# Down projection of a decoder block as seven block products with a three-slot ring

## The chip, the cores and the metric

The kernel runs on one core of one Trainium2 chip. The metric is the time of one execution in microseconds (us) on the device. The engines are TensorE (PE, with its weight loads PEld), VectorE (DVE), ScalarE (ACT), GpSimd (POOL) and SyncE (SP), whose queue issues nearly all DMAs here.

## What is computed

A decoder block on 2048 tokens of width 1024: two mixers side by side, one output projection, then a SwiGLU feed-forward with 2816 hidden columns and a last norm. The part at hand, all in float32:

```python
h = h + jnp.concatenate([y_a, y_b], axis=-1) @ w_out[l]
u = rmsnorm(h, ln2_g[l])
h = h + (jax.nn.silu(u @ w_gate[l]) * (u @ w_up[l])) @ w_down[l]
return rmsnorm(h, final_g)
```

## The kernel before

Tokens go in four blocks (it) of 512 through the mixers. The feed-forward works on pairs (p) of such blocks, so on 1024 tokens; the program order is `ffn(0), down, down, ffn(1), down, down`.

**Precision.** Every float32 product is three matmuls: each operand is split into a rounded part (hi, written by ScalarE) and the rest (lo, written by VectorE as raw minus hi), and hi x hi, lo x hi and hi x lo are added up in a PSUM bank.

**Gate and up (`ffn`).** For each of 22 iterations g of a pair (even g gate, odd g up, so 11 gate-and-up pairs j) the product of a 256-column block of the weights with the 1024 tokens is built from seven block products (A11, A12, S2, S1, S3, S4, A22) of 12 matmuls each. GpSimd forms the sums of weight blocks. ScalarE and VectorE split the weights of a product three products ahead (LEAD): after product o of g they handle the weights of product o + 3. VectorE and ScalarE read the banks into four quarters, gq0 to gq3 for gate, au0 to au3 for up; ScalarE applies silu to gq, VectorE multiplies au by gq, and SP stores au into the DRAM scratch a_scr.

**Down (`down(it)`).** For each of the four 512-token blocks, 22 rows k are taken in order. A row has 128 rows of w_down (1024 columns, 512 KB, dw_raw) and the activations that go with them (512 tokens, 256 KB, da_raw), and gives 24 matmuls: four groups of 128 tokens by two halves of columns, so all eight PSUM banks. Three buffers of each kind form a ring (CRING = 3). SP loads row rr into its slot when TensorE has finished row rr - 3 (`load_row`, the wait on s_row); ScalarE writes the hi parts (`row_hi`), VectorE the lo parts (`row_lo`), both two rows ahead in their programs; TensorE waits for lo. Between rows SP loads the operands of the next pair's gate and up from u_scr, 1 MB each, and in the next rows VectorE combines and splits them. After the 22 rows eight additions bring the banks into the residual (`residual`), and squares, their sum, a root and a scaling give the output.

**Order.** Nothing is scheduled by a planner: each engine's program is written out by these functions, engines run in order, and semaphores join them. A waiting instruction holds up all behind it on its engine.

## Time and profile before

| | us |
|---|---|
| median of 3 runs | 2338.1 |
| lowest, highest | 2337.46, 2338.29 |
| the profiled execution | 2335.22 |
| its span, first to last instruction | 2333.5 |
| mixers, up to about | 1000 |
| gate and up, first pair, up to | 1411.76 |
| down, first pair, up to | 1657.59 |
| gate and up, second pair, up to | 2078.87 |
| down, second pair, last matmul | 2321.81 |

The profile is one execution, taken by the hardware profiler. Matmuls overlap one another, so the time of a stretch is read from starts, not from durations. Idle time of an engine that nobody waits for costs nothing. In the rows below SPq is SP's DMA queue, and a bracket at the end of a row says how long the engine sat idle before it and what ended that.

### The profile page before, as it was taken

What the parts mean: (1) busy time and instruction counts of PE and PEld (TensorE: products, weight loads), DVE (VectorE), ACT (ScalarE), POOL (GpSimd) and SP (SyncE); (2) the same over time, 40 slices, a digit from 0 to 9 for tenths busy, and PEclk for the clock granted to TensorE, in tenths of its full rate; (3) what the DMA queues carried; (4) which work ended last, traced back from release to release, by engine and by line L of the source; (5) the groups of instructions that cost most, each with busy time, mean ns of one, the idle gap of its engine ahead of it and who ended that gap; (6) DMA issues with size and microseconds to landing.
All of it is one profiled execution on the core that took longest, in us unless ns stands there. A gap on an engine that the chain in (4) does not pass through costs nothing.

```text
span 2333.5 us, 29887 instructions
## 1 busy us (share of the span) xinstructions
PE 2272.5 (97%) x11336; PEld 1886.6 (81%) x11336; DVE 1355.0 (58%) x2047; ACT 981.0 (42%) x1727; POOL 478.4 (21%) x376
## 2 busy tenths in 40 slices
PE   6999999999999999899999999999999999999998
PEld 5888788878887888678888888778888888888786
DVE  5775588557865786656554544753555555543444
ACT  4554545444544554443333333532433333332422
POOL 1230223122222122332222320000222223200000
PEclk9999999999999999999999999999999999999999
DMA  4222332233323323523232216646232222235463
GB/s 118 83 81 81 109 110 92 94 104 118 96 86 106 103 89 117 183 73 113 86 127 73 91 55 245 229 136 235 90 105 82 93 84 84 81 109 192 138 212 126
DMA packets 217854, 269.87 MB, mean 116 GB/s; under 512 B 12784, under 2 KB 164336, under 8 KB 214896
## 3 DMA queue, kind: packets, MB, share of 16 engines
q1 hardware_dynamic: 215408, 259.58, 33.8%
q10 hardware_dynamic: 2304, 8.39, 0.9%
q8 instruction: 91, 1.49, 0.3%
q14 instruction: 51, 0.42, 0.1%
HBM read 219.69 MB, written 48.23 MB: 115 GB/s over the span
## 4 chain that ended last, share of the span: by engine, by line
PE 81%; DVE 7%; issue 3%; ACT 3%; DMA 3%; POOL 1%; SPq 1%; ACTq 0%; DVEq 0%; POOLq 0%
PE M L1050 9%; PE M L1052 9%; PE M L1051 9%; PE M L758 7%; PE M L760 6%; PE M L759 6%; PE M L1080 3%; PE M L1082 3%; PE M L1081 3%; PE X L1081 3%; PE X L1080 3%; PE X L1082 3%; PE X L1050 3%; PE X L1052 3%; PE X L1051 2%
## 5 line engine op out<-in xcount | busy, mean ns | idle before, releaser
L1536 DVE TENSOR_TENSOR wlo<-raw,whi 128x1024 fp32r<-128x1024 f32 x120 | 161.8, 1348 | 216.9 <-ACT whi L1110 216.9
L758 PE MATMUL M<-uhi,whi 128*128 128x512 f32 x704 | 283.9, 403 | 1.7 <-DVE ulo L1558 1.5
L760 PE MATMUL M<-uhi,wlo 128*128 128x512 f32 x704 | 275.4, 391 | 0.0
L759 PE MATMUL M<-ulo,whi 128*128 128x512 f32 x704 | 274.8, 390 | 0.0
L1950 DVE TENSOR_TENSOR dw_lo<-dw_raw,dw_hi 128x1024 fp32r<-128x1024 f32 x88 | 108.0, 1228 | 263.2 <-ACT dw_hi L1443 262.9
L1050 PE MATMUL M<-t_hi,wu_hi 128*128 128x512 f32 x616 | 240.1, 390 | 1.6 <-DVE wu_lo L1871 0.9
L1052 PE MATMUL M<-t_hi,wu_lo 128*128 128x512 f32 x616 | 240.0, 390 | 0.0
L1051 PE MATMUL M<-t_lo,wu_hi 128*128 128x512 f32 x616 | 239.7, 389 | 0.0
L1443 ACT ACTIVATE dw_hi<-dw_raw 128x1024 fp32r<-128x1024 f32 x88 | 93.3, 1061 | 313.0 <-DMA dw_raw<-in_w_down_dram 309.8
L1871 DVE TENSOR_TENSOR wu_lo<-fraw,wu_hi 128x512 fp32r<-128x512 f32 x132 | 133.1, 1018 | 111.6 <-ACT wu_hi L1386 111.2
L1110 ACT ACTIVATE whi<-raw 128x1024 fp32r<-128x1024 f32 x120 | 126.6, 1055 | 156.4 <-PE M L760 140.2
L2088 POOL TENSOR_TENSOR pr<-pr,rd 128x512 f32<-128x512 f32 x64 | 84.4, 1318 | 386.6 <-DVE rd L1569 386.6
L758 PEld LDWEIGHTS M<-uhi,whi 128*128 128x128 f32 x704 | 132.6, 188 | 32.5 <-issue 6.2
L760 PEld LDWEIGHTS M<-uhi,wlo 128*128 128x128 f32 x704 | 132.5, 188 | 28.7
L759 PEld LDWEIGHTS M<-ulo,whi 128*128 128x128 f32 x704 | 132.9, 189 | 25.7 <-issue 0.7
L1080 PE MATMUL M<-dw_hi,da_hi 128*128 128x512 f32 x352 | 137.5, 391 | 8.5 <-DVE da_lo L1950 4.5
L2154 POOL TENSOR_TENSOR fs<-fraw 128x512 f32<-128x512 f32 x44 | 58.4, 1328 | 411.7 <-DMA fraw<-in_w_gate_dram 207.3
L2160 POOL TENSOR_TENSOR fraw<-fraw,fs 128x512 f32<-128x512 f32 x44 | 57.4, 1304 | 409.9 <-DVE wl_lo L1871 409.8
L1871 DVE TENSOR_TENSOR wu_lo<-fs,wu_hi 128x512 fp32r<-128x512 f32 x88 | 61.2, 696 | 134.5 <-ACT wu_hi L1386 133.5
L1050 PEld LDWEIGHTS M<-t_hi,wu_hi 128*128 128x128 f32 x616 | 115.6, 188 | 26.9 <-DVE wu_lo L1871 2.1
L1082 PE MATMUL M<-dw_hi,da_lo 128*128 128x512 f32 x352 | 137.0, 389 | 0.0
L1081 PE MATMUL M<-dw_lo,da_hi 128*128 128x512 f32 x352 | 137.0, 389 | 0.0
(271 smaller groups left out, 5252.2 us busy)
## 6 DMA issues: line engine op xcount, KB each, us to landing
raw<-in_w_in_dram SPq DMA_DIRECT2D x88, 512.0 KB, 3.8
dw_raw<-in_w_down_dram SPq DMA_DIRECT2D x88, 512.0 KB, 3.7
fraw<-in_w_gate_dram SPq DMA_DIRECT2D x44, 512.0 KB, 4.6
fraw<-in_w_up_dram SPq DMA_DIRECT2D x44, 512.0 KB, 4.8
a_scr<-au SPq DMA_DIRECT2D x88, 256.0 KB, 2.0
da_raw<-a_scr SPq DMA_DIRECT2D x88, 256.0 KB, 3.9
raw<-in_w_out_dram SPq DMA_DIRECT2D x32, 512.0 KB, 3.8
xs<-in_x_dram SPq DMA_DIRECT2D x32, 256.0 KB, 4.1
```

Of the source, the lines that this page charges most:

```text
L758: mm(bank, whi[s][:, kb, :], hi, start=first, stop=False)
L759: mm(bank, whi[s][:, kb, :], lo, start=False, stop=False)
L760: return mm(bank, wlo[s][:, kb, :], hi, start=False, stop=last)
L1050: mm(bank[:, :], wh[:, k, :], hi[:, k, :], start=start and k == 0, stop=False, skip_group_check=True)
L1051: mm(bank[:, :], wh[:, k, :], lo[:, k, :], start=False, stop=False, skip_group_check=True)
L1052: last = mm(bank[:, :], wl[:, k, :], hi[:, k, :], start=False, stop=k == KH - 1, skip_group_check=True)
L1080: mm(DBANKS[n][:, :], ahi_k[:, tokens], whi_k[:, cols], start=k == 0, stop=False)
L1081: mm(DBANKS[n][:, :], ahi_k[:, tokens], wlo_k[:, cols], start=False, stop=False)
L1082: last = mm(DBANKS[n][:, :], alo_k[:, tokens], whi_k[:, cols], start=False, stop=k == KF - 1)
L1110: A(whi[s][:, :, :], raw[s][:, :, :], ACT.Copy).then_inc(s_hi[s], 1)
L1536: V.tensor_tensor(wlo[s][:, :, :], raw[s][:, :, :], whi[s][:, :, :].bitcast(F32), ALU.subtract).then_inc(s_lo[s], 1)
L1871: V.tensor_tensor(wl[:, :, :], ffn_part(g, o), wh[:, :, :].bitcast(F32), ALU.subtract).then_inc(s_flo, 1)
```

## The change

Down is computed for the 1024 tokens of a pair at once, with seven block products q in place of eight: two token halves by two column halves of the result, and w_down's 22 blocks of 128 rows taken as 11 pairs (j). Product q takes 11 rows, so a pair has 77 rows of 12 matmuls. A row is one 128x512 half block of weights (256 KB) and one 512-token block of activations (256 KB), side by side in one ring slot (ring0 to ring2), which ScalarE and VectorE each split with one instruction of 128x1024. There are still three slots.

- The activations' sums that the products need are formed in gate and up by VectorE: two after au2's product, two after au3's, written over gq1, gq2, au2 and gq3, and stored by SP. a_scr holds seven blocks for each j.
- The weights' combinations are formed once, in the first pair's `ffn`: from g = 10 on SP loads one 1 MB block of w_down (tw) after each g, VectorE makes four in-place sums in the next g (`t_step`, behind products A11, S2 and S1), and SP stores it into t_scr. From product 2 on, both pairs read weights from t_scr.
- TensorE writes a product into four banks, in two sets in turn. Banks are not cleared for every product (BEGINS); each product's banks are added into the residual during the next product (`residual`), four additions of 128x512 for each of seven products.
- The residual is loaded in 16 pieces of 256 KB, and the next pair's operands in 28 pieces of 256 KB in place of 7 loads of 1 MB, one at most behind a row. Squares, root, scaling and stores of the first 512 tokens of a pair are done before the last row.

```diff
+TARGET = ((0, 0), (0, 0), (0, 1), (1, 1), (1, 1), (0, 1), (1, 0))
+BEGINS = (0, 1, 3)
+WEIGHT_HALF = ((False, 0, 0), (False, 1, 0), (True, 0, 0), (True, 0, 1), (True, 1, 1), (False, 1, 1), (True, 1, 0))
+SQUARED = ((0, 0), (1, 1), (0, 1), (1, 0))
+SQUARED_WITH = (1, 4, 5, 6)
+PIECES = (("r", 0), "T3", "T1", ("r", 2), "T2", ("r", 1), "T4", "B11", "B21", ("r", 3), "B22")
+COMBINE_AT = {27: 0, 38: 1, 41: 2, 49: 3}
+SPLIT_AT = {51: "B11", 54: "B21", 59: "T2", 61: "T1", 63: "T3", 70: "B22", 75: "T4"}
...
+    a_scr = nc.dram_tensor("a_scr", [NPAIR, PRODUCTS, NJ, P, T], F32, kind="Internal").ap()
+    t_scr = nc.dram_tensor("t_scr", [KF, P, D], F32, kind="Internal").ap()
+    w_down_2 = w_down.rearrange("o (j k p) d -> (o j) p k d", k=2, p=P)
...
-        DW = [pair_at("dw0", stage_at, stage_at + 4 * K, (P, D)), pair_at("dw1", y_at + 4 * K, y_at + 8 * K, (P, D)),
-              pair_at("dw2", whi_at + 4 * K, wlo_at + 4 * K, (P, D))]
-        DA = [pair_at("da0", g1_at + 2 * K, spare_at, (P, T)), pair_at("da1", snap_at, snap_at + 2 * K, (P, T)),
-              pair_at("da2", gu_at, gu_at + 2 * K, (P, T))]
-        res = [at(f"res{b}", (P, D), kk_at + 4 * K * b) for b in range(TB)]
+        RING = [pair_at(f"ring{i}", o, o + 4 * K, (P, 2, T)) for i, o in enumerate((stage_at, y_at + 4 * K, snap_at))]
+        res = [[at(f"res0{b}", (P, D), o) for b, o in enumerate((dist_at, whi_at + 4 * K, wlo_at + 4 * K, gu_at))],
+               [at(f"res1{b}", (P, D), kk_at + 4 * K * b) for b in range(TB)]]
         gfrow = at("gfrow", (P, D), y_at + 28 * K)
-        dump = [snap[1], acc_last]
+        dump = acc_last
+        tw = [at(f"tw{i}", (P, 2, D), kk_at + 8 * K * i) for i in range(2)]
...
+        def banks_of(p, g):
+
+            return BANKS[(p + g) % 2]
+
+        def down_banks(p, q):
+
+            return BANKS[(p + q) % 2] + (X[2 + (p + q) % 2],)
...
-                sp.dma_start(OPERAND[o][2][:, :, :], u_scr[2 * p + n, :, k0:k0 + KH, :]).then_inc(s_opl[o], 16)
+                for k in range(KH) if part is None else (part,):
+                    sp.dma_start(OPERAND[o][2][:, k, :], u_scr[2 * p + n, :, k0 + k, :]).then_inc(s_opl[o], 16)
...
+                sp.dma_start(a_scr[p, (0, 6, 4, 1)[n], j, :, :], au[n][:, :]).then_inc(s_ast[n], 16)
+
+            def store_s(p, j, n):
+
+                sp.wait_ge(s_au, 7 * (p * NJ + j) + (4, 5, 7)[n])
+                sp.dma_start(a_scr[p, (3, 2, 5)[n], j, :, :], gq[1 + n][:, :]).then_inc(s_sst, 16)
+
+            def load_t(j):
+
+                if j < 2:
+                    sp.wait_ge(s_ust, 32 * NSB)
+                else:
+                    sp.wait_ge(s_ts, 16 * (j - 1))
+                sp.dma_start(tw[j % 2][:, :, :], w_down_2[j, :, :, :]).then_inc(s_tl, 16)
+
+            def store_t(j):
+
+                sp.wait_ge(s_tc, 4 * j + 4)
+                sp.dma_start(t_scr_2[j, :, :, :], tw[j % 2][:, :, :]).then_inc(s_ts, 16)
...
-                it, k = 2 * p + rr // KF, rr % KF
+                q, j = divmod(rr, NJ)
                 if rr >= CRING:
-                    sp.wait_ge(s_row, p * 2 * KF + rr - CRING + 1)
+                    sp.wait_ge(s_row, p * NR + rr - CRING + 1)
...
+                ring = RING[rr % CRING][2]
+                combined, k, half = WEIGHT_HALF[q]
+                if combined:
...
+                sp.dma_start(ring[:, 0, :], (t_scr if combined else w_down_k)[2 * j + k, :, half * T:(half + 1) * T]
+                             ).then_inc(s_ring[rr % CRING], 16)
...
+                sp.dma_start(ring[:, 1, :], a_scr[p, q, j, :, :]).then_inc(s_ring[rr % CRING], 16)
...
+                    if p == 0 and g >= T_LOAD + 2:
+                        store_t(g - T_LOAD - 2)
...
                         store_a(p, j, 1)
                         if last:
                             load_row(p, 1)
+                            load_row(p, 2)
+                        store_s(p, j, 0)
+                        store_s(p, j, 1)
                         store_a(p, j, 2)
                         store_a(p, j, 3)
+                        store_s(p, j, 2)
                     if p == 0 and g == 9:
                         store_u(NSB - 1, 0)
                         store_u(NSB - 1, 1)
-
...
+                    if p == 0 and 0 <= g - T_LOAD < NJ:
+                        load_t(g - T_LOAD)
+                if p == 0:
+                    store_t(NJ - 1)
...
+            def down(p):
+                pieces = {}
+                for i in range(TB * len(PIECES)):
+                    pieces[CRING + i * 29 // 20] = (PIECES[i // TB], i % TB)
+                for rr in range(CRING, NR):
+                    load_row(p, rr)
+                    if rr in pieces:
+                        what, part = pieces[rr]
+                        if what in OPERAND_NAMES:
+                            if p + 1 < NPAIR:
+                                load_operand(p + 1, OPERAND_NAMES[what], part)
+                        else:
+                            m, half = SQUARED[what[1]]
+                            load_res(p, m, part, half)
+                    if rr == 45:
                         for n in (2, 3):
                             sp.wait_ge(s_ast[n], 16 * NJ * (p + 1))
                         sp.dma_start(gfrow[:, :], final_g.partition_broadcast(P)).then_inc(s_gf, 16)
-                    if it % 2 and k == 9:
-                        store_out(it - 1)
-                    if k == 10:
-                        load_res(it)
-                    if it % 2 and k == 12 and p + 1 < NPAIR:
-                        load_ffn(p + 1, 0)
+                    if p + 1 < NPAIR and rr in (67, 70):
+                        load_ffn(p + 1, 0, (int(rr == 70),))
+                    if rr >= NR - 2:
+                        store_out(p, 0, rr - NR + 2)
+                for b in range(2, TB):
+                    store_out(p, 0, b)
...
+            def down(p):
+                for rr in range(NR):
+                    q, j = divmod(rr, NJ)
+                    banks = down_banks(p, q)
+                    pe.wait_ge(s_rowlo, NR * p + rr + 1)
+                    hi, lo, _ = RING[rr % CRING]
+                    for b in range(TB):
+                        if j == 0:
+                            wait_bank_read(pe, p, q, b)
+                        tokens = slice(b * P, (b + 1) * P)
+                        first, last = j == 0 and q in BEGINS, j == NJ - 1
+                        mm(banks[b][:, :], hi[:, 1, tokens], hi[:, 0, :], start=first, stop=False, skip_group_check=True)
+                        mm(banks[b][:, :], hi[:, 1, tokens], lo[:, 0, :], start=False, stop=False, skip_group_check=True)
+                        done = mm(banks[b][:, :], lo[:, 1, tokens], hi[:, 0, :], start=False, stop=last,
+                                  skip_group_check=True)
+                        if last and b < TB - 1:
+                            done.then_inc(s_bank, 1)
+                    done.then_inc(s_row, 1)
...
+                act.wait_ge(s_ring[rr % CRING], 32 * row_loads(p, rr))
+                hi, _, raw_r = RING[rr % CRING]
+                A(hi[:, :, :], raw_r[:, :, :], ACT.Copy).then_inc(s_rowhi, 1)
...
+                                dve.wait_ge(s_au, 7 * j + 3)
+                                V.tensor_tensor(gq[1][:, :], au[2][:, :], au[1][:, :], ALU.add).then_inc(s_au, 1)
+                                dve.wait_ge(s_au, 7 * j + 4)
+                                V.tensor_tensor(gq[2][:, :], gq[1][:, :], au[0][:, :], ALU.subtract).then_inc(s_au, 1)
...
+                            V.tensor_tensor(au[2][:, :], au[0][:, :], au[2][:, :], ALU.subtract).then_inc(s_au, 1)
+                            dve.wait_ge(s_au, 7 * j + 5)
+                            dve.wait_ge(s_c21[1], j + 1)
+                            V.tensor_tensor(gq[3][:, :], au[3][:, :], gq[2][:, :], ALU.subtract).then_inc(s_au, 1)
+                        if p == 0 and T_LOAD < g <= T_LOAD + NJ:
+                            t_step(g - T_LOAD - 1, o)
...
+            def t_step(j, o):
+
+                top, bottom = (tw[j % 2][:, k, :] for k in range(2))
+                left, right = slice(0, T), slice(T, 2 * T)
+                if o == 0:
+                    dve.wait_ge(s_tl, 16 * (j + 1))
+                    V.tensor_tensor(bottom[:, right], bottom[:, right], top[:, right], ALU.subtract).then_inc(s_tc, 1)
+                if o == 2:
+                    dve.wait_ge(s_tc, 4 * j + 1)
+                    V.tensor_tensor(top[:, right], top[:, right], top[:, left], ALU.subtract).then_inc(s_tc, 1)
+                if o == 3:
+                    dve.wait_ge(s_tc, 4 * j + 2)
+                    V.tensor_tensor(top[:, left], top[:, left], bottom[:, right], ALU.add).then_inc(s_tc, 1)
+                    dve.wait_ge(s_tc, 4 * j + 3)
+                    V.tensor_tensor(bottom[:, left], bottom[:, left], top[:, left], ALU.subtract).then_inc(s_tc, 1)
...
+                hi, lo, raw_r = RING[rr % CRING]
+                dve.wait_ge(s_rowhi, NR * p + rr + 1)
+                V.tensor_tensor(lo[:, :, :], raw_r[:, :, :], hi[:, :, :].bitcast(F32), ALU.subtract).then_inc(s_rowlo, 1)
...
+            def residual(p, q, b):
+                m, half = TARGET[q]
+                cols = slice(half * T, (half + 1) * T)
+                if q in BEGINS + (2, 6) and q != 1 and b == 0:
+                    dve.wait_ge(s_ht[m ^ half], 128 * p + 64 * (m + 1))
+                if b < TB - 1:
+                    dve.wait_ge(s_bank, (TB - 1) * (PRODUCTS * p + q) + b + 1)
+                else:
+                    dve.wait_ge(s_row, NR * p + NJ * (q + 1))
+                if q in (1, 4, 5):
+                    dve.wait_ge(s_res, NADD * p + TB * {1: 0, 4: 3, 5: 2}[q] + b + 1)
+                V.tensor_tensor(res[m][b][:, cols], res[m][b][:, cols], down_banks(p, q)[b][:, :],
+                                ALU.add).then_inc(s_res, 1)
...
+            def down(p):
+                for rr in range(NR):
+                    q, j = divmod(rr, NJ)
+                    if rr + 2 < NR:
...
+                    if q and j < TB:
+                        residual(p, q - 1, j)
...
+                    if p + 1 < NPAIR and rr in COMBINE_AT:
+                        combine(p + 1, (T3, T1, T2, T4)[COMBINE_AT[rr]])
+                    if p + 1 < NPAIR and rr in SPLIT_AT:
+                        op_lo(p + 1, OPERAND_NAMES[SPLIT_AT[rr]])
```

The order changes in two places that matter for what follows. The first is VectorE in gate and up of the first pair, from the end of an up iteration to the next gate (g = 12). Names ending in _lo are splits of weights, fs and fraw hold weights, snap is a bank's copy. Before:

```order
L1915 TENSOR_TENSOR au2_179<-au2_179,gq2_175 128x512 [waits s_silu,s_blk]
L1871 TENSOR_TENSOR wu0_lo_188<-fs1_163,wu0_hi_187 128x512 [waits s_fhi]
L1921 TENSOR_TENSOR au3_180<-M3,gq3_176 128x512 [waits s_ast3,s_c210,s_prod]
L1871 TENSOR_TENSOR wu1_lo_191<-fs0_162,wu1_hi_190 128x512 [waits s_fhi]
L1889 TENSOR_TENSOR gq0_173<-M1,snap0_168 128x512 [waits s_snap,s_prod]
L1871 TENSOR_TENSOR wu2_lo_194<-fraw0_164,wu2_hi_193 128x512 [waits s_fhi]
L1871 TENSOR_TENSOR wu0_lo_188<-fraw0_164,wu0_hi_187 128x512 [waits s_fhi]
L1871 TENSOR_TENSOR wu1_lo_191<-fraw0_164,wu1_hi_190 128x512 [waits s_fhi]
L1899 TENSOR_TENSOR gq1_174<-M0,snap2_170 128x512 [waits s_snap,s_prod]
```

Now:

```order
L1985 TENSOR_TENSOR au2_179<-au2_179,gq2_175 128x512 [waits s_silu,s_blk]
L1987 TENSOR_TENSOR gq1_174<-au2_179,au1_178 128x512 [waits s_au]
L1989 TENSOR_TENSOR gq2_175<-gq1_174,au0_177 128x512 [waits s_au]
L1937 TENSOR_TENSOR wu0_lo_188<-fs1_163,wu0_hi_187 128x512 [waits s_fhi]
L1995 TENSOR_TENSOR au3_180<-M3,gq3_176 128x512 [waits s_ast3,s_c210,s_prod]
L1996 TENSOR_TENSOR au2_179<-au0_177,au2_179 128x512
L1999 TENSOR_TENSOR gq3_176<-au3_180,gq2_175 128x512 [waits s_c211,s_au]
L1937 TENSOR_TENSOR wu1_lo_191<-fs0_162,wu1_hi_190 128x512 [waits s_fhi]
L2032 TENSOR_TENSOR tw1_215<-tw1_215 128x512 [waits s_tl]
L1957 TENSOR_TENSOR gq0_173<-M1,snap0_168 128x512 [waits s_snap,s_prod]
L1937 TENSOR_TENSOR wu2_lo_194<-fraw0_164,wu2_hi_193 128x512 [waits s_fhi]
L1937 TENSOR_TENSOR wu0_lo_188<-fraw0_164,wu0_hi_187 128x512 [waits s_fhi]
```

Four sums came in, and the first sum of tw stands ahead of the gate's gq0 and of the split of weights for S3 (wu2_lo). The load it waits for stands here on SP's queue, from the stores of g = 17 to the load of the next block:

```order
L630 DMA a_scr<-gq2_175 128x512 [waits s_au]
L625 DMA a_scr<-au2_179 128x512 [waits s_au]
L625 DMA a_scr<-au3_180 128x512 [waits s_c211]
L630 DMA a_scr<-gq3_176 128x512 [waits s_au]
L638 DMA tw1_215<-in_w_down_dram 128x2x1024 [waits s_ts]
L643 DMA t_scr<-tw0_214 128x2x1024 [waits s_tc]
L587 DMA fraw0_164<-in_w_gate_dram 128x4x256 [waits s_flo]
L587 DMA fraw0_164<-in_w_gate_dram 128x4x256
L638 DMA tw0_214<-in_w_down_dram 128x2x1024 [waits s_ts]
```

The load of tw1 comes after the last store of the odd iteration, the load of tw0 after the even iteration's weights; before the change the L638 and L643 rows and the L630 rows were not there.

The second place is SP's queue within the down stage of the first pair (dw and da are the row's two loads). Before, two rows and what lies between them:

```order
L615 DMA dw1_raw_201<-in_w_down_dram 128x1024 [waits s_row]
L625 DMA da1_raw_210<-a_scr 128x512 [waits s_ast3]
L615 DMA dw2_raw_204<-in_w_down_dram 128x1024 [waits s_row]
L625 DMA da2_raw_213<-a_scr 128x512 [waits s_ast0]
L591 DMA b11_raw_143<-u_scr 128x2048 [waits s_prod]
L615 DMA dw0_raw_198<-in_w_down_dram 128x1024 [waits s_row]
L625 DMA da0_raw_207<-a_scr 128x512 [waits s_ast3]
L615 DMA dw1_raw_201<-in_w_down_dram 128x1024 [waits s_row]
L625 DMA da1_raw_210<-a_scr 128x512 [waits s_ast0]
```

Now:

```order
L662 DMA ring0_raw_198<-in_w_down_dram 128x512 [waits s_row]
L669 DMA ring0_raw_198<-a_scr 128x512 [waits s_ast3]
L662 DMA ring1_raw_201<-in_w_down_dram 128x512 [waits s_row]
L669 DMA ring1_raw_201<-a_scr 128x512 [waits s_ast3]
L616 DMA t3_raw_155<-u_scr 128x512 [waits s_prod]
L662 DMA ring2_raw_204<-in_w_down_dram 128x512 [waits s_row]
L669 DMA ring2_raw_204<-a_scr 128x512 [waits s_ast3]
L616 DMA t1_raw_152<-u_scr 128x512 [waits s_prod]
L662 DMA ring0_raw_198<-in_w_down_dram 128x512 [waits s_row]
L669 DMA ring0_raw_198<-a_scr 128x512 [waits s_ast3]
L662 DMA ring1_raw_201<-in_w_down_dram 128x512 [waits s_row]
L669 DMA ring1_raw_201<-a_scr 128x512 [waits s_ast3]
```

A row's two loads are now of one size, and a piece of 256 KB (here of the operand t1) follows two rows of three, where a load of 1 MB followed every second row.

## Rows read from the trace of the kernel before

**Rows 1.** page, busy time, share of the span and instructions of each engine

```profile
PE 2272.5 (97%) x11336; PEld 1886.6 (81%) x11336; DVE 1355.0 (58%) x2047; ACT 981.0 (42%) x1727; POOL 478.4 (21%) x376
```

**Rows 2.** windows: stretch, length, busy by engine, PEclk, DMA share, GB/s; FFN, down, down

```profile
1000.00:1411.50 411.50, 410.42 (x1821) 339.29 (x1822) 225.39 (x276) 151.94 (x262) 113.26 (x82) 1.00 0.28 92
...
1411.76:1657.59 245.83, 240.31 (x1058) 198.00 (x1057) 120.97 (x122) 89.45 (x114) 6.42 (x4) 1.00 0.57 199
2078.87:2321.81 242.94, 239.95 (x1057) 197.91 (x1055) 93.48 (x108) 78.52 (x113) 0.00 (x0) 1.00 0.50 167
```

**Rows 3.** timeline, TensorE, down stages: start, length, engine, line, operation

```profile
1515.15 0.39 PE L1080 MATMUL X<-dw_hi,da_hi 128*128 128x512 f32 x1
...
1521.95 0.39 PE L1080 MATMUL M<-dw_hi,da_hi 128*128 128x512 f32 x1
...
1657.59 0.39 PE L1050 MATMUL M<-b_hi,wl_hi 128*128 128x512 f32 x1
...
2321.58 0.39 PE L1082 MATMUL M<-dw_hi,da_lo 128*128 128x512 f32 x1
```

**Rows 4.** timeline, all engines, one ring slot from its row's end to its split

```profile
1516.97 0.39 PE L1082 MATMUL M<-dw_hi,da_lo 128*128 128x512 f32 x1
...
1517.39 0.33 SPq L615 DMA_DIRECT2D dw_raw<-in_w_down_dram  x1
...
1517.76 0.43 SPq L625 DMA_DIRECT2D da_raw<-a_scr  x1
...
1521.41 1.06 ACT L1443 ACTIVATE dw_hi<-dw_raw 128x1024 fp32r<-128x1024 f32 x1 [4.38 <-DMA dw_raw<-in_w_down_dram]
...
1522.51 1.23 DVE L1950 TENSOR_TENSOR dw_lo<-dw_raw,dw_hi 128x1024 fp32r<-128x1024 f32 x1 [4.14 <-ACT dw_hi L1443]
```

**Rows 5.** timeline, VectorE and TensorE, a down row that was waited for

```profile
1472.78 0.68 DVE L1950 TENSOR_TENSOR da_lo<-da_raw,da_hi 128x512 fp32r<-128x512 f32 x1
...
1473.52 0.50 PE L1080 MATMUL M<-dw_hi,da_hi 128*128 128x512 f32 x1 [1.75 <-DVE da_lo L1950]
...
1474.32 0.40 PE L1080 MATMUL M<-dw_hi,da_hi 128*128 128x512 f32 x1
```

**Rows 6.** DMA of dw_raw, issue to landing (512 KB, 4 KB rows), 88 loads

```profile
DMA to landing us min/median/max: 3.4/3.7/9.6
```

**Rows 7.** loads of raw at 911.3, w_out, 512 KB in 2 KB rows, alone

```profile
L528 SPq DMA_DIRECT2D raw<-in_w_out_dram x1: 378/378/378, 911.3 to 911.3; - x1
...
DMA to landing us min/median/max: 3.8/3.8/3.8
```

**Rows 8.** the same at 919.2, with three loads of xs behind it

```profile
L528 SPq DMA_DIRECT2D raw<-in_w_out_dram x1: 368/368/368, 919.2 to 919.2; - x1
...
DMA to landing us min/median/max: 4.7/4.7/4.7
```

**Rows 9.** load of xs at 928.5, 256 KB in 2 KB rows

```profile
L539 SPq DMA_DIRECT2D xs<-in_x_dram x1: 328/328/328, 928.5 to 928.5; - x1
...
DMA to landing us min/median/max: 2.7/2.7/2.7
```

**Rows 10.** timeline, VectorE, from an up product to the next gate

```profile
1296.92 1.35 DVE L1915 TENSOR_TENSOR au<-au,gq 128x512 f32<-128x512 f32 x1
...
1301.47 0.69 DVE L1871 TENSOR_TENSOR wu_lo<-fs,wu_hi 128x512 fp32r<-128x512 f32 x1 [1.86 <-ACT wu_hi L1386]
...
1303.77 1.74 DVE L1871 TENSOR_TENSOR wu_lo<-fraw,wu_hi 128x512 fp32r<-128x512 f32 x1
```

**Rows 11.** DMA of b_raw, issue to landing (1 MB)

```profile
DMA to landing us min/median/max: 5.0/7.1/9.5
```

**Rows 12.** timeline, TensorE, first matmul of the gate's S3

```profile
1308.30 0.39 PE L1050 MATMUL M<-t_hi,wu_hi 128*128 128x512 f32 x1
```

**Rows 13.** timeline, VectorE and ScalarE, the end of the program

```profile
2322.01 0.69 DVE L1962 TENSOR_TENSOR res<-res,M 128x512 f32<-128x512 f32 x1
...
2323.75 0.63 ACT L1454 ACTIVATE acc_last<-res 128x512 f32<-128x512 f32 x1
```

323 lines of the change are left out of this document (139 added, 184 removed).

## The prediction

> **What bounds the kernel now.** I read the page's first part, then the windows of the stages, then the order of time inside one down row. TensorE is busy 97% of the span [rows 1]; in the FFN window of the first pair 410.42 of 411.50 us, in the two down windows 240.31 of 245.83 and 239.95 of 242.94 [rows 2]. So the kernel goes by the number of matmuls. Their pace in the down stage is read between two starts that are 30 matmuls apart, 1515.15 and 1521.95 [rows 3]: 0.2267 us each (the "mean ns" of 390 is pipelined and is no cost). A down row of 24 matmuls takes 5.44 us. The two down windows are 245.83 + 242.94 = 488.8 us; 2112 matmuls at 0.2267 are 478.9, the other 9.9 are waits.
>
> The second thing to read is what one ring slot goes through, because a slot may only be loaded again when its row is finished [rows 4]. The row's last matmul starts at 1516.97, SP issues the next load into the slot at 1517.39 (0.42 later), the second load 0.37 after it; ScalarE starts on the landed data at 1521.41, VectorE 1.10 later, for 1.23 us. In before this chain has two rows of 5.44 us to hide in, and it does: even with the 0.68 of the second split [rows 5], 0.42 + 4.02 + 1.10 + 1.23 + 0.68 = 7.5 is under 10.9.
>
> **The change, part by part.**
>
> *Matmuls removed.* Down goes from 4 x 22 rows of 24 to 2 x 77 rows of 12: 2112 to 1848. 264 fewer at 0.2267 are 59.9 us, and the 9.9 us of waits go too if nothing replaces them. The ideal is 209.5 us for each pair.
>
> *The ring turn.* The ring still has three slots, but a row now takes 12 x 0.2267 = 2.72 us, so the chain has 5.44 us to hide in, half of what it had. Its length, from one first matmul to the first matmul of the same slot's next row: 11 matmuls to the last one, 2.49; a row that was waited for starts slower, 0.80 instead of 0.68 over its first three matmuls [rows 5], 0.12; to the issue 0.42 [rows 4]; landing L; ScalarE to VectorE 1.10 (the shape stays 128x1024); VectorE 1.23; VectorE's end to the matmul 0.06 (1472.78 + 0.68 to 1473.52) [rows 5]. Together 5.42 + L for three rows. With the matmuls alone three rows take 8.16, so every L over 2.74 shows.
>
> L is now the landing of two loads of 256 KB, issued 0.37 apart, which ScalarE waits for together. No row shows just this. One load of 512 KB in 4 KB rows lands in 3.7 us in the median [rows 6]; one of 512 KB in 2 KB rows, which is what the new loads have, lands in 3.8 with nothing around it [rows 7] and in 4.7 with more loads queued right behind [rows 8]; one of 256 KB lands in 2.7 [rows 9], so the pair can't be under 2.7 + 0.37 = 3.1. I take 3.7, since amount and width are those of [rows 6, 7], and keep 3.1 and 4.4 (between [rows 7] and [rows 8]) as ends. A turn is then 9.12 us, a row 3.04 instead of 2.72.
>
> For each pair: row 1 starts late. After the last up product VectorE now does three sums (au3, au2, gq3) of 0.69 before it can split row 1 for 1.23 us, so that row starts about 3.6 us after row 0 instead of 2.72. Then 25 turns of 9.12 bring row 76, and its own 2.84: 3.6 + 228.0 + 2.84 = 234.4 us.
>
> *What is laid between the rows.* In the first pair 44 loads of 256 KB stand behind rows on SP's queue, 28 of them operand pieces; in the second 16. By [rows 7] against [rows 8] a load queued behind costs up to 0.9 us; these are smaller and come once in a turn or twice, so 0.4 each on one of three slots: 44 x 0.4 / 3 = 5.9 and 16 x 0.4 / 3 = 2.1 us (ends 0 and 13). The 11 combines and operand splits on VectorE (about 2.3 us beside a split of 1.23, in a row of 3.04) delay one slot by 0.5 each: 5.5 at most, 2.5 with what the other slots absorb. Before row 3 of the first pair SP has the last 1 MB store of t_scr in its queue: 2. Residual sums (0.69) and squares fit into a row. The bank sets cost nothing, since each bank is added into the residual a whole product before it is written again. Pair 0: 234.4 + 5.9 + 2.5 + 2 = 244.8. Pair 1: 234.4 + 2.1 = 236.5. Together 481.3, **7.5 us less** than 488.8.
>
> *Sums in gate and up.* Four VectorE sums of 128x512 for each of 22 gate-and-up pairs, 0.69 each, up to 1.74 where GpSimd runs [rows 10]. VectorE waits 1 to 2 us several times in each such pair (1.86 in one case) [rows 10] and splits are three products (8.2 us) ahead, so I cost them at nothing; without that cover it is 1 us or so a time, 22 in all (a rival below). The store of the sums delays SP's other loads by 1 or 2 us, and those have over 10 us.
>
> *The combination of w_down (first pair, 11 blocks).* Its load of 1 MB is issued at the end of an iteration. After an odd g that is very late: VectorE's multiplication ends at 1298.27 [rows 10], then come two sums, a split, au3, au2, gq3 at 0.67 each, to 1302.3; SP stores gq3 and issues the load at about 1302.8. Yet VectorE asks for it right after its first split of the next g, at 1303.0, and **it stands in order**: behind it wait the gate sum and the split of the weights of S3. I take 5.5 us to land: 1 MB loads took 5.0 at least and 7.1 in the median [rows 11], here with a 256 KB store ahead and a 1 MB store behind, but no rows. Landed at 1308.3, three operations of 0.69 and 0.18 to the matmul give 1310.5, where S3 started at 1308.30 [rows 12]: 2.2 us of TensorE. After an even g the load stands behind the weights' load, which goes out in the middle of g, so it has landed by the next g. Blocks 1, 3, 5, 7 and 9 are late: 5 x 2.2 = **11 us more** (ends 8 for a landing in 5.0, 19 for 7.1).
>
> *Tail.* Before, the last square starts 1.05 us after the end of the last sum (2322.01 + 0.69 to 2323.75) [rows 13], since eight queue up; now four: 0.6 less.
>
> **The sum.** -7.5 + 11 - 0.6 = +2.9. The profiled execution took 2335.2 us (span 2333.5), 2.9 below the median of 2338.1; so 2338.1 for a profiled execution, 2341 in the median. The 264 matmuls are paid back by the ring turns and five waits.
>
> The Trainium skill (DMA: Bandwidth & Descriptors, section on the anatomy of one DMA) fits a transfer as 2.0 us plus its bytes over 436 GB/s, on the path issued from GpSimd. That is 3.2 us for 512 KB where [rows 6, 7] show 3.7 and 3.8, so the trace doesn't agree; an estimate by that page would make a turn 8.6 us and the whole about 2316, inside the first rival.
>
> **Rivals.**
> *Short landing (faster).* Two loads side by side land in 3.1, [rows 9] being the model. A turn is 8.53, a pair 3.6 + 213.3 + 2.84 = 219.7; with the 12.5 of extras 451.9; 36.9 less, and 2311.6 in the median. For it: 256 KB alone took 2.7. Against it: of 88 loads of 512 KB the fastest took 3.4 [rows 6]. The forecast turns to faster (by over 0.2%) from L = 3.55 down.
> *Long landing (slower).* A queue that moves 512 KB every 3 us, with pieces, makes L 4.4. A turn is 9.82, a pair 251.9, together 508.3 with the pieces counted at 4.5; +19.5 + 10.4, 2368. For it: [rows 8], and that DMA has a share of 0.5 in the down windows already [rows 2]. Against: in most rows nothing else is in flight when a slot is issued.
> *No ring limit at all.* L is 2.7, each pair 209.5 + 0.9 and 5 of extras for both: 425.8, 63.0 less; + 10.4 gives 2285.5.
> *The w_down load doesn't stall.* The forecast without its 11 us: 2330.
> *VectorE is late in every gate-and-up pair.* One us for each of 22: 2363.
>
> **How the numbers follow.** Forecast 0.35 (2331 to 2351), short landing 0.27 (2300 to 2325), long landing 0.22, no ring limit 0.04, no stall 0.04, VectorE late 0.08. About 0.2% is what a measurement of this kernel can tell from no change. Faster: 0.27 + 0.04 + 0.04 and 0.04 of the forecast, 0.39. Same: 0.18 of the forecast. Slower: 0.13 of it, 0.22 and 0.08, 0.43. The range 2306 to 2368 leaves out 0.2: the lowest rival (0.04), the lower end of the short landing (0.06) and the upper half of the long one (0.10).
>
> **What would show it.** In the profile after: down rows 3.0 us apart with a gap before each row's first matmul put down to VectorE's split, SP's load issues in the same distance; the two down stages at some 245 and 237 us; five waits of VectorE for the load of tw, and TensorE late in the same g. Rows 2.8 us apart mean the short landing, 3.2 or more the long one; no gap at all breaks the ring argument. If VectorE's wait for tw is there but TensorE has no gap, the split was not needed then.

## The result, and the profile after

The changed kernel takes **2374.97 us** (median of 4 runs, 2372.46 to 2384.19), the kernel before 2337.78 in the same series: a ratio of 1.0167 [1.0151, 1.0184]. It is 1.7% slower. The forecast was 2341 with a range up to 2368, so time and range were both missed. The profiled span is 2375.1 us, where before had 2333.5: 41.6 more.

The page's first line, and the windows of the four stages (stretch, length, then busy us and instructions of TensorE, weight load, VectorE, ScalarE, GpSimd, then PEclk, DMA share, GB/s). They answer to [rows 1] and [rows 2]; the two down stages are the second and the fourth:

```profile
PE 2255.5 (95%) x11072; PEld 1840.6 (77%) x11072; DVE 1458.9 (61%) x2181; ACT 1003.5 (42%) x1705; POOL 478.3 (20%) x376
```

```profile
985.30:1441.30 456.00, 436.75 (x1883) 357.80 (x1884) 279.33 (x368) 163.21 (x275) 127.62 (x89) 0.97 0.46 152
1441.30:1700.50 259.20, 229.92 (x926) 173.45 (x925) 138.62 (x122) 103.35 (x112) 4.68 (x3) 0.97 0.66 220
1700.50:2121.30 420.80, 419.94 (x1850) 346.93 (x1849) 242.22 (x316) 157.85 (x274) 119.05 (x85) 1.00 0.31 106
2121.30:2364.00 242.70, 223.29 (x925) 170.44 (x923) 116.27 (x113) 90.43 (x105) 0.00 (x0) 0.99 0.59 195
```

TensorE's busy time in the down stages fell (240.31 to 229.92, 239.95 to 223.29), yet the first stage is longer than in before, 259.2 for 245.8, and the second is level, 242.7 for 242.9. Most of the loss is in the first line. Gate and up of the first pair took 428.8 us in before (983.0 to 1411.8, from first matmul to first matmul of down) and take 456.0 now, 27.2 more. The gate-and-up stage of the second pair is unchanged (421.3 and 420.8). The 41.6 are 27.2 + 13.4 - 0.2 - 0.5, 2.3 by which the first stage begins later, and -0.6 at the end.

**Where the 27.2 are.** The waits between 1000 and 1441 (who waited for whom, us in total, times, longest), and one late block of w_down in the timeline. In the timelines here rows of other engines between the rows shown are left out; dots stand for further rows.

```profile
DVE tw L2032 <- DMA tw<-in_w_down_dram: 36.5, 5, 8.0
...
PE M L1116 <- DVE wu_lo L1937: 18.8, 6, 4.2
```

```profile
1272.27 0.45 SPq L638 DMA_DIRECT2D tw<-in_w_down_dram  x1
1272.76 0.65 SPq L643 DMA_DIRECT2D t_scr<-tw  x1
...
1279.40 0.69 DVE L2032 TENSOR_TENSOR tw<-tw 128x512 f32<-128x512 f32 x1 [7.29 <-DMA tw<-in_w_down_dram]
...
1281.35 0.80 PE L1116 MATMUL M<-t_hi,wu_hi 128*128 128x512 f32 x1 [3.50 <-DVE wu_lo L1937]
1281.94 0.63 PE L1117 MATMUL M<-t_lo,wu_hi 128*128 128x512 f32 x1
1282.36 0.63 PE L1118 MATMUL M<-t_hi,wu_lo 128*128 128x512 f32 x1
1282.79 0.63 PE L1116 MATMUL M<-t_hi,wu_hi 128*128 128x512 f32 x1
```

Five waits, in order on VectorE, with TensorE behind them (its gaps are 3.2, 3.5, 4.2, 3.2 and 3.4 us; the sixth wait in the row, 1.2 us, is at 1003 and stands in kernel 1 below too): this is the mechanism of the forecast. Two things are larger. The load lands 7.1 us after its issue, not 5.5 (6.8 to 7.8 for the five late blocks), and right behind it stands the 1 MB store of the block before. And after the gap the matmuls start 0.427 us apart instead of 0.227: TensorE runs at 1.2 GHz instead of 2.4. Two windows of that place, before and behind the gap:

```profile
1260.00:1270.00 10.00, 10.00 (x46) 8.28 (x45) 8.68 (x13) 2.19 (x4) 1.29 (x1) 1.00 0.48 159
1281.40:1288.00 6.60, 6.60 (x18) 5.26 (x19) 4.09 (x7) 0.63 (x1) 0.00 (x0) 0.58 0.58 181
```

In 6.6 us there are 18 matmuls where 29 fit at 2.4 GHz, and the granted clock is 0.58 (the low stretch ends inside the window). A busy engine hides this: the 456.00 us hold 436.75 of TensorE's busy time for the same 1883 matmuls that take 427.08 where no wait stands (below). So of the 27.2, 9.7 are matmuls at the lower clock, and the rest, 17.5 or 3.5 for each late block, is idle time.

**The ring.** One turn of a slot in the second pair, which answers to [rows 4]; after the row's first matmul the last, SP, ScalarE, VectorE, and the first matmul of the slot's next row:

```profile
2199.70 0.50 PE L1144 MATMUL M<-ring_hi 128*128 128x512 f32 x1 [0.60 <-DVE ring_lo L2045]
...
2202.35 0.39 PE L1146 MATMUL X<-ring_hi,ring_lo 128*128 128x512 f32 x1
...
2202.77 0.32 SPq L662 DMA_DIRECT2D ring_raw<-t_scr  x1
2203.13 0.43 SPq L669 DMA_DIRECT2D ring_raw<-a_scr  x1
...
2206.48 1.06 ACT L1509 ACTIVATE ring_hi<-ring_raw 128x1024 fp32r<-128x1024 f32 x1 [2.97 <-DMA ring_raw<-a_scr]
...
2207.58 1.23 DVE L2045 TENSOR_TENSOR ring_lo<-ring_raw,ring_hi 128x1024 fp32r<-128x1024 f32 x1 [2.21 <-ACT ring_hi L1509]
...
2208.86 0.50 PE L1144 MATMUL M<-ring_hi 128*128 128x512 f32 x1 [0.53 <-DVE ring_lo L2045]
```

2.65 + 0.42 + 3.71 + 1.10 + 1.28 = 9.16 us for this turn: the forecast's 9.12, and its L of 3.7. Over the 52 rows loaded between 2135 and 2300 the time from SP's first issue to ScalarE's start has a mean of 3.68 (3.22 to 4.69); in the first pair, between 1466 and 1600, it is 4.00 for 41 rows (3.22 to 5.83).

**The start of a down stage.** Rows 3 and 4 of the first pair come 6.85 and 5.29 us after the rows before them. SP's queue there, and who waits:

```profile
1444.75 0.49 SPq L643 DMA_DIRECT2D t_scr<-tw  x1
1445.28 0.64 SPq L662 DMA_DIRECT2D ring_raw<-in_w_down_dram  x1
1445.96 1.18 SPq L669 DMA_DIRECT2D ring_raw<-a_scr  x1
1451.78 0.32 SPq L684 DMA_DIRECT2D res<-ht_scr  x1
1452.15 0.42 SPq L662 DMA_DIRECT2D ring_raw<-in_w_down_dram  x1
...
1452.87 1.06 ACT L1509 ACTIVATE ring_hi<-ring_raw 128x1024 fp32r<-128x1024 f32 x1 [5.79 <-DMA ring_raw<-a_scr]
...
1455.23 0.79 PE L1144 MATMUL M<-ring_hi 128*128 128x512 f32 x1 [3.83 <-DVE ring_lo L2045]
```

Row 3's load stands behind five stores of 256 KB (activations and their sums) and the 1 MB store of t_scr, and ScalarE starts on it 7.6 us after its issue (1445.28 to 1452.87). SP's waits between 1435 and 1465 have this row, ahead of the first residual piece (L684):

```profile
SPq L677 <- DMA t_scr<-tw: 4.4, 1, 4.4
```

SP waits until the store of t_scr has landed, and row 4's load waits behind that. But in this trace it isn't what makes row 4 late. Row 4's split and first matmul:

```profile
1457.75 1.23 DVE L2045 TENSOR_TENSOR ring_lo<-ring_raw,ring_hi 128x1024 fp32r<-128x1024 f32 x1 [2.57 <-ACT ring_hi L1509]
...
1460.52 0.63 PE L1144 MATMUL M<-ring_hi 128*128 128x512 f32 x1
```

The split is done 1.5 us before TensorE comes to it, without a gap. The 5.29 us are row 3's twelve matmuls at 0.427 us: behind the gap of 3.83 the granted clock is at half from 1454.2 to 1461.0. In the second pair rows 3 and 4 come after 5.14 and 5.06 us, with gaps of 2.20 and 0.45 and a half clock of 3.4 us.

**The end of a down stage.** Rows 69 to 71 of the first pair come 3.5 to 4.6 us apart, row 72 5.4. ScalarE and VectorE there (acc_last is the square of a residual block):

```profile
1674.88 0.63 ACT L1519 ACTIVATE acc_last<-res 128x512 f32<-128x512 f32 x1 [2.90 <-DVE res L2058]
...
1675.51 1.04 ACT L1509 ACTIVATE ring_hi<-ring_raw 128x1024 fp32r<-128x1024 f32 x1
...
1676.59 1.23 DVE L2045 TENSOR_TENSOR ring_lo<-ring_raw,ring_hi 128x1024 fp32r<-128x1024 f32 x1 [1.74 <-ACT ring_hi L1509]
1677.73 0.68 DVE L2058 TENSOR_TENSOR res<-res,X 128x512 f32<-128x512 f32 x1
...
1678.45 0.63 ACT L1519 ACTIVATE acc_last<-res 128x512 f32<-128x512 f32 x1 [1.89 <-DVE res L2058]
```

A circle of 3.57 us (1674.88 to 1678.45): the square waits for the residual sum, the sum stands behind the row's split on VectorE, the split waits for ScalarE's rounding of the row, and that stands behind the square before. Loads play no part in it. Row 72 (a gap of 2.35 us) comes when an operand's split stands in both programs behind row 70, and row 73, 4.29 us later without a gap, is half clock again, from 1682.9 on.

### The profile page after: what moved, and what is told of

Read it like the earlier page. It is cut to its first block, busy times and chain, and to the rows that moved or that the text cites. A ratio compares the mean times of both kernels' runs of the same rounds, so it can differ in the third digit from the quotient of the medians.

```text
span 2375.1 us, 29898 instructions
## 1 busy us (share of the span) xinstructions
PE 2255.5 (95%) x11072; PEld 1840.6 (77%) x11072; DVE 1458.9 (61%) x2181; ACT 1003.5 (42%) x1705; POOL 478.3 (20%) x376
## 4 chain that ended last, share of the span: by engine, by line
PE 67%; DVE 11%; DMA 9%; ACT 5%; issue 4%; SPq 2%; POOL 1%; ACTq 0%; DVEq 0%; POOLq 0%
PE M L1116 8%; PE M L1118 8%; PE M L1117 8%; DMA ring_raw<-a_scr 7%; PE M L824 7%; PE M L826 6%; PE M L825 6%; PE X L1118 2%; PE X L1117 2%; PE X L1116 2%; DVE ring_lo L2045 2%; ACT ring_hi L1509 2%; PE M L1144 2%; DMA tw<-in_w_down_dram 1%; PE M L932 1%
## 5 line engine op out<-in xcount | busy, mean ns | idle before, releaser
L2045 DVE TENSOR_TENSOR ring_lo<-ring_raw,ring_hi 128x1024 fp32r<-128x1024 f32 x154 | 189.6, 1231 | 246.5 <-ACT ring_hi L1509 246.4
L1509 ACT ACTIVATE ring_hi<-ring_raw 128x1024 fp32r<-128x1024 f32 x154 | 163.0, 1059 | 299.6 <-DMA ring_raw<-a_scr 296.4
L1118 PE MATMUL M<-t_hi,wu_lo 128*128 128x512 f32 x616 | 242.9, 394 | 0.0
L1937 DVE TENSOR_TENSOR wu_lo<-fraw,wu_hi 128x512 fp32r<-128x512 f32 x132 | 123.6, 947 | 97.8 <-ACT wu_hi L1452 97.4
L1144 PE MATMUL M<-ring_hi 128*128 128x512 f32 x308 | 132.7, 431 | 48.7 <-DVE ring_lo L2045 47.7
L1117 PEld LDWEIGHTS M<-t_lo,wu_hi 128*128 128x128 f32 x616 | 117.6, 191 | 24.6
L1118 PEld LDWEIGHTS M<-t_hi,wu_lo 128*128 128x128 f32 x616 | 117.5, 191 | 24.7
L1144 PEld LDWEIGHTS M<-ring_hi 128*128 128x128 f32 x308 | 58.8, 191 | 96.9 <-DVE ring_lo L2045 87.2
```

The costliest lines, as they stand in the source:

```text
L1117: mm(bank[:, :], wh[:, k, :], lo[:, k, :], start=False, stop=False, skip_group_check=True)
L1118: last = mm(bank[:, :], wl[:, k, :], hi[:, k, :], start=False, stop=k == KH - 1, skip_group_check=True)
L1144: mm(banks[b][:, :], hi[:, 1, tokens], hi[:, 0, :], start=first, stop=False, skip_group_check=True)
L1509: A(hi[:, :, :], raw_r[:, :, :], ACT.Copy).then_inc(s_rowhi, 1)
L1937: V.tensor_tensor(wl[:, :, :], ffn_part(g, o), wh[:, :, :].bitcast(F32), ALU.subtract).then_inc(s_flo, 1)
L2045: V.tensor_tensor(lo[:, :, :], raw_r[:, :, :], hi[:, :, :].bitcast(F32), ALU.subtract).then_inc(s_rowlo, 1)
```

## Experiments

Each kernel ran for 3 rounds beside before (2337.6, 2336.7, 2335.8 and 2337.2 us in the four series).

**1. The load of tw after an odd g goes out before the iteration's stores of activations, a good half iteration earlier (block 1 at 1217.64 and not 1228.96).**

```diff
                             load_ffn(p, g + 2)
+                        if p == 0 and 0 <= g - T_LOAD < NJ:
+                            load_t(g - T_LOAD)
                         store_a(p, j, 1)
...
-                    if p == 0 and 0 <= g - T_LOAD < NJ:
+                    if p == 0 and g % 2 == 0 and 0 <= g - T_LOAD < NJ:
                         load_t(g - T_LOAD)
```

> The changed kernel, with only the load of w_down's block (tw) after odd iterations issued earlier in SP's program: behind the next up weights' load, ahead of the stores of the iteration. Theory (VectorE stands in order at five late tw loads, TensorE's next split comes late, and its clock falls behind these gaps): the five waits of VectorE go, gate and up of the first pair falls from 456 us to 430 (before: 429), TensorE's granted clock there is 1.00, and the time is 2350. Rival (the eight added sums of a gate-and-up pair overload VectorE): gate and up stays at 445 or more, 2365.

Measured: 2344.94 us, ratio 1.0033 [1.0021, 1.0045]. The windows of gate and up and of down in the first pair:

```profile
984.60:1413.40 428.80, 427.08 (x1883) 352.42 (x1884) 283.23 (x368) 162.59 (x275) 130.88 (x89) 0.99 0.47 162
1413.40:1668.90 255.50, 225.83 (x926) 170.46 (x925) 137.67 (x122) 103.36 (x112) 5.85 (x3) 0.99 0.67 223
```

The stage is back at the 428.8 of before, with all additions and all 44 sums of tw still in it. So the whole 27.2 was the late load; the sums themselves cost nothing, as forecast, and the half clock in that stage goes with the gaps. The time is 5 us under the 2350 expected; another 3.7 are in down of the first pair, where executions of this same program differ by 2 (255.5 here, 253.4 in kernel 6).

**2. No combinations of w_down at all.** Load, sums and store of tw are left out, and products 2 to 6 read w_down's own rows, so the result is another.

```diff
-                        if p == 0 and T_LOAD < g <= T_LOAD + NJ:
-                            t_step(g - T_LOAD - 1, o)
...
-                sp.dma_start(ring[:, 0, :], (t_scr if combined else w_down_k)[2 * j + k, :, half * T:(half + 1) * T]
+                sp.dma_start(ring[:, 0, :], w_down_k[2 * j + k, :, half * T:(half + 1) * T]
```

> The changed kernel without the combination of w_down: no load, sum or store of tw and t_scr; the down rows of products 2 to 6 (but one) read uncombined w_down blocks of the same shape, so the output leaves the weights' combinations out. The activations' sums stay. Theory (late tw loads are the whole loss in gate and up): first pair's gate and up 430 us, the same as with the early load within 2; time 2348. Rival (the activations' sums or their stores cost there too): 435 us or more, and more than with the early load taken away from it.

Measured: 2341.64, ratio 1.002 [1.0011, 1.003]. Gate and up 428.8 as in 1; down of the first pair 251.6, 3.9 less than in 1. Of that 3.9, 2.6 are in rows 0 to 6 (21.3 us instead of 23.9), where the last 1 MB store of t_scr is gone from the queue; the other 1.3 is no more than two executions of one program differ by. The gate-and-up stage is as expected and the rival's 435 is out; the time is 6 us under the 2348 expected.

**3. A fourth ring slot.** The tile os is free in down; two waits are added where the slot is first loaded and where os is next written, and the residual pieces keep their rows.

```diff
-CRING = 3
+CRING = 4
...
-enumerate((stage_at, y_at + 4 * K, snap_at))]
+enumerate((stage_at, y_at + 4 * K, snap_at, os_at))]
```

> The changed kernel with a fourth slot in the ring of down rows (8 KB of buffer that is free in down), loads issued three rows ahead instead of two. Theory (a row waits for one slot's turn: load, two splits, matmuls, 9.3 us for three rows): with four slots a turn may take 10.9 us, so rows go at 2.72 to 2.80 us; down 259 and 242 us fall to 218 and 215, time 2305. Rival (the DMA engines, at a share of 0.66 in down, or VectorE can't deliver a row every 2.72 us): rows stay at 3.0 or more and the two stages over 235, time over 2355.

Measured: 2315.08, ratio 0.9905 [0.989, 0.992]. Windows:

```profile
984.40:1440.40 456.00, 436.04 (x1882) 357.33 (x1883) 279.36 (x368) 163.14 (x275) 127.64 (x89) 0.98 0.45 152
1440.40:1664.80 224.40, 213.93 (x926) 173.88 (x925) 137.75 (x122) 103.10 (x112) 4.80 (x3) 0.99 0.77 254
1664.80:2085.60 420.80, 419.94 (x1850) 346.95 (x1849) 242.43 (x316) 157.84 (x274) 119.05 (x85) 1.00 0.31 106
2085.60:2304.40 218.80, 213.33 (x925) 173.99 (x923) 116.25 (x113) 90.33 (x105) 0.00 (x0) 0.99 0.66 218
```

The stages lose 34.8 and 23.9 us, and gate and up stay at 456.0. From row 6 to row 68 the rows run 2.72 to 2.73 us apart in the mean, the pace of the matmuls, although the mean time from issue to ScalarE's start is no shorter (4.09 and 3.88 us): with four slots the chain has 8.2 us to hide in. That is the ring argument, shown by its removal. DMA was not at its limit either: it moved 254 GB/s here and 220 in the changed kernel. The expected 2305 was missed by 10 us, since the stages were put at 218 and 215: rows 3 and 4 and the last ones of a stage are still late with four slots.

**4. Both edits, 1 and 3.**

> The early tw load and the fourth ring slot together. Theory: both losses are separate, so the gains add up: 2375 - 26 - 68 = 2281, under the kernel before by 2.4%. Rival (with the matmuls no longer held up, DMA traffic or VectorE turns up as the next limit): 2310 or more.

Measured: 2287.36, ratio 0.9783 [0.9767, 0.9799]; the four stages 428.8, 226.2, 420.8, 217.0. The gains add up to within 2.3 us: 30.0 and 59.9 us alone, 87.6 together (the expected 2281 had taken the slot's gain for 68). What is left over 209.5 is 16.7 and 7.5 us, at the rows that were late in the profile after: 3 and 4 (7.00 and 5.29; 5.0 and 5.2 in the second pair) and 69 to 73.

**5. Only the store behind the late load is held back** until the load has landed; the load stays late.

```diff
+                        if g % 2 == 0:
+                            sp.wait_ge(s_tl, 16 * min(NJ, g - T_LOAD))
                         store_t(g - T_LOAD - 2)
```

> The changed kernel; only the store of a finished tw block in an even half, which stood on SP's queue directly behind the load of the next block, now waits until that load has landed. Theory A (the stall is the landing of the load, and the 1 MB store queued right behind it makes it 7 to 8 us instead of 5.4): the five late loads land in 5.2 to 5.6, each wait of VectorE falls from 7.3 to about 5.3, the first gate and up stage from 456.0 us to 440 to 447, and the stretches of half clock in it get fewer; whole kernel 2360 to 2367. Theory B (the landing is long by itself; a load of 1 MB beside 256 KB stores takes 7.7): the stage stays at 456 and the kernel at 2375. Theory C (the clock is the main part and comes back only when no gap is left): landings fall, but the stage stays over 450.

Measured: 2361.15, ratio 1.0101 [1.0083, 1.0118]. The block that was shown above, and the stage's window:

```profile
1268.41 0.45 SPq L638 DMA_DIRECT2D tw<-in_w_down_dram  x1
1274.05 0.37 SPq L643 DMA_DIRECT2D t_scr<-tw  x1
...
1274.06 0.69 DVE L2034 TENSOR_TENSOR tw<-tw 128x512 f32<-128x512 f32 x1 [5.81 <-DMA tw<-in_w_down_dram]
```

```profile
984.60:1427.30 442.70, 429.71 (x1883) 352.68 (x1883) 279.21 (x368) 163.19 (x275) 127.66 (x89) 0.99 0.46 157
```

This load lands in 5.65 us. Over the five late loads the landing is 5.4 to 6.0 us (mean 5.6) where the changed kernel had 6.8 to 7.8 (mean 7.1). Theory A holds in the stage, the time and the fewer stretches of half clock, one for four; its landings (5.2 to 5.6) and waits of VectorE (about 5.3, measured 5.6 to 6.8) were put somewhat low. B and C are out. The idle time over kernel 1's is (442.70 - 429.71) - (428.80 - 427.08) = 11.3 us, 2.25 a block; the busy time over it is 2.6, where the changed kernel had 9.7. A stall shorter by 1.3 us costs 2.7 less a block, because most of the low clock goes with it.

**6. Operand-sized loads in the second pair too.** To kernel 1 are added 28 loads of 256 KB behind rows 3 to 42 of the last down stage, to tiles that nobody reads any more.

```diff
                             if p + 1 < NPAIR:
                                 load_operand(p + 1, OPERAND_NAMES[what], part)
+                            else:
+                                sp.wait_ge(s_prod, NQ * NPAIR)
+                                sp.dma_start(OPERAND[OPERAND_NAMES[what]][2][:, part, :],
+                                             u_scr[2 * p, :, part, :]).then_inc(s_dummy, 16)
```

> The kernel with the early load of tw, and in the second pair's down stage 28 loads of 256 KB behind rows 3 to 42, in the places in which the first pair loads operand pieces (they go to the same tiles and nobody reads them). Down of the second pair took 242.9 us, of the first 255.5. Theory A (the operand pieces on SP's queue make the landing of rows longer, which is what the first pair has over the second): the second stage rises to 250 to 256, rows 3.2 to 3.3 us apart instead of 3.11; whole kernel 2352 to 2358. Theory B of the prediction's size (0.4 us on one of three slots, 28 x 0.13): 246 to 247, whole kernel 2349. Theory C (VectorE's combinations and operand splits, the store of t_scr and the clock make the difference): stays at 243, 2345.

Measured: 2347.97, ratio 1.0049 [1.003, 1.0068]; from the first to the last matmul's start the last down stage is 1.9 us longer than in 1 (244.5 for 242.6), with no stretch of low clock in either. That is little over what executions of one program differ by in this stage (242.6 in the changed kernel and in 1, 243.4 in 5). The forecast had 3.7 for the 28 pieces. The pieces do lengthen the landing: between 2108 and 2250 the mean time from issue to ScalarE's start is 3.95 us and 3.68 in 1, so most of what the first pair's 4.00 has over 3.68 goes to them. The difference of 13 us between the pairs is mostly something else; what it is stays open, with VectorE's combinations and splits and the clock left untried.

**7. The first residual pieces behind rows 5 to 8** instead of 3 to 7, on kernel 1.

```diff
+                pieces = {(5, 6, 7, 8)[i] if i < 4 else 4 + i * 29 // 20: (PIECES[i // TB], i % TB)
+                          for i in range(TB * len(PIECES))}
```

> The kernel with the early load of tw; in both pairs the first four residual pieces are loaded behind rows 5 to 8 instead of 3 to 7, the other pieces one row later. Theory A (SP waits at the first residual piece until all stores of the sums have landed, and the load of row 4 stands behind that wait; so row 4 starts 2 us late): the gap of row 4 falls from 5.1 to 5.3 us to 3.0 to 3.5 in both pairs, each down stage 1.5 to 2 us shorter, whole kernel 2341 to 2342. Theory B (the slot's own chain and the queued stores make row 4 late, the wait is hidden in them): both down stages and 2345 stay.

Measured: 2343.97, ratio 1.003 [1.0021, 1.004], the same as 1. Row 4 of the second pair now comes 2.85 us after row 3 (it was 3.95), in the first pair 4.20 (4.92), but both stages are no shorter (258.2 and 243.7). The first pair says little: TensorE's gap before row 4 was only 0.3 us in kernel 1, the rest of its 4.92 us half clock, and the profiled execution was the slowest of ten (2349.45 us), with two more stretches of half clock in that stage than kernel 1, 3.4 us each. In the second pair there is none, and rows 0 to 6 take 20.4 us for 20.5: row 4's gap of 0.9 us goes, but row 6 comes 3.56 us after row 5 and not 2.72. So the wait makes row 4 late, as theory A has it, but by less than A's 2 us, and the stage and the time stay, as B has it. I read this as the ring setting the pace whenever a row is early; that was not isolated. Only a kernel whose ring is not the bound can tell what the start is worth, which is the next one.

**8. Both of 4, and the last stores of activations and sums one at a time behind rows 3 to 7**, the last store of t_scr behind row 8, pieces from row 9 on. Five of the operand splits stand one to four rows later, since their pieces come later.

```diff
+                stores = {3: (store_s, 0), 4: (store_s, 1), 5: (store_a, 2), 6: (store_a, 3), 7: (store_s, 2)}
...
                     load_row(p, rr)
+                    if rr in stores:
+                        stores[rr][0](p, NJ - 1, stores[rr][1])
+                    if rr == 8 and p == 0:
+                        store_t(NJ - 1)
```

> Early load of tw and four slots as in the kernel that took 2287.4 us, and the five stores of the last sums, which stood between the loads of row 2 and row 3, go one at a time behind the loads of rows 3 to 7, the store of the last tw block behind row 8, the residual and operand pieces from row 9 on. Theory A (the stores in front make rows 3 and 4 late, 7.0 and 5.3 us in the first pair, 5.0 and 5.2 in the second, where 2.72 is the pace of the matmuls): these rows come 2.8 to 3.3 us apart, the stages fall from 226.2 and 217.1 to 218 to 221 and 213 to 214, whole kernel 2273 to 2279. Theory B (the first rows are late because of VectorE's sums, not because of the queue): the two stages lose under 3 us together, 2285.

Measured: 2281.52, ratio 0.9763 [0.9749, 0.9778]; stages 222.4 and 212.1. Rows 3 to 6 come 2.72 or 2.73 us apart in both pairs, so the queue made them late and not VectorE's sums, which are still there. In the first pair rows 0 to 6 take 17.2 us for 25.0, but only 3.8 us are gained in the stage and not 5 to 8: rows 9 to 11, behind the 1 MB store, now come 3.3 to 3.5 apart, and rows 66 to 76 take 36.2 for 34.4 (why was not followed). The time lies between the two theories' (2279 at most and 2285).

**9. The squares one row later**, with their sum and root, and the scaling two rows later, on kernel 4.

```diff
-                    if q == 6 and j < TB:
-                        out_square(p, 2 * TB + j)
+                    if q == 6 and 1 <= j <= TB:
+                        out_square(p, 2 * TB + j - 1)
```

> As the kernel that took 2287.4 us (early load of tw, four slots), only the four squares of the last product and what follows from them (sum, root, scaling) stand one row later in the program of ScalarE and VectorE, the root's reciprocal and the scaling two rows later. Theory A (rows 69 to 71 are a circle: ScalarE's square waits for VectorE's residual sum, that stands behind the row's split on VectorE, the split waits for ScalarE's rounding of the row, and that stands behind the square before; 0.63 + 1.04 + 1.23 + 0.68 us, which is the 3.6 us between rows): rows 69 to 71 come 2.73 to 2.9 us apart instead of 3.56 to 3.61 in the first pair and rows 71 and 72 instead of 3.30 and 3.57 in the second; the operand split behind row 72 of the first pair still costs 1 to 2.6 us; stages 2.5 and 1.5 us shorter, whole kernel 2283 to 2284. Theory B (the loads of the ring are late there, because outputs and gate weights share the queue): the gaps stay, 2287.

Measured: 2292.39, ratio 0.9812 [0.9795, 0.983], slower than 4 and than either theory's time. The circle is gone, as theory A has it: rows 69 to 75 come 2.72 to 2.76 us apart in both pairs, also past the operand split. But row 76 comes 6.5 us after row 75 in both. VectorE and then SP's queue there, in the first pair:

```profile
1624.00 1.28 DVE L2080 SCALAR_TENSOR_TENSOR res<-res,rnrm,gfrow 128x1024 f32<-128x1024 f32 x1
```

```profile
1625.31 0.34 SPq L690 DMA_DIRECT2D out_dram<-res  x1
1625.75 0.70 SPq L664 DMA_DIRECT2D ring_raw<-t_scr  x1
```

The store of output 0 waits for the scaling, which the edit had moved, and row 76's load stands behind the store.

**10. The same edit on kernel 8:**

> The kernel that took 2281.5 us (early load of tw, four slots, stores of the sums behind rows 3 to 8) with the later squares as well. If the start of the down stage and the circle of the squares are separate costs, this takes 2.5 + 1.5 us off again: 2277 to 2278. If one hid the other, it stays at 2281.

Measured: 2285.33, ratio 0.9781 [0.976, 0.9803], 3.8 over kernel 8, with the same late row 76 (7.16 and 6.53 us), which neither expected time had in it.

**11. The first two outputs are stored behind the load of row 76**, on kernel 9, and **12.** on kernel 10.

```diff
-                    if rr >= NR - 2:
-                        store_out(p, 0, rr - NR + 2)
-                for b in range(2, TB):
+                for b in range(TB):
                     store_out(p, 0, b)
```

> As the kernel with the later squares and early stores of the sums (2292.4 us), only the first two outputs of a pair are stored behind the load of row 76 instead of one before and one behind it. There rows 69 to 75 ran 2.72 to 2.75 us apart, but row 76 came 6.5 us late, since its load stood on SP's queue behind the store of output 0 (issued 1625.31), which waited for VectorE's scaling. Theory A: row 76 comes 2.73 to 2.9 us after row 75, both stages 3.7 us shorter, whole kernel 2284 to 2285 (and 2283 if the clock stays up). Theory B (the load of row 76 is late from something else, the slot or the queue): row 76 stays at 6 us or more and the kernel at 2292.

> The same edit on the kernel of 2285.3 us that also spreads the stores of the sums. If the start of the stage, the squares and the outputs are separate, the stages are 216 to 218 and 211 to 212, 2277 to 2278 in all; if the gain is taken by something behind the stages (the first weights of the next stage), it stays at 2281 or over.

Measured: 2280.24, ratio 0.9755 [0.9739, 0.9772], and **2275.01**, ratio 0.973 [0.9715, 0.9744]. Row 76 comes after 2.73 us in both, and both times are 2 to 5 us under the expected ones. The last kernel's four stages:

```profile
985.60:1413.80 428.20, 426.37 (x1883) 351.70 (x1882) 283.58 (x369) 161.69 (x274) 130.50 (x89) 1.00 0.47 163
1413.80:1629.60 215.80, 212.35 (x925) 172.85 (x925) 138.07 (x123) 103.12 (x112) 5.31 (x3) 1.00 0.80 262
1629.60:2050.40 420.80, 419.94 (x1849) 346.94 (x1849) 241.87 (x317) 157.84 (x275) 120.38 (x85) 1.00 0.32 107
2050.40:2261.10 210.70, 210.00 (x923) 172.85 (x921) 115.15 (x111) 89.91 (x103) 0.00 (x0) 1.00 0.68 223
```

The down stages stand at 215.8 and 210.7 where 924 matmuls at 0.2267 are 209.5, and no stretch of low clock is left in them. This kernel is 2.7% faster than before and 4.2% faster than the changed one, with the same arithmetic: what the change lacked was in the order of SP's queue and of two engines' programs, and one more slot.

## Why the prediction was wrong

The ring turn and the late loads of tw worked as forecast. The sum failed where it had a term too small or at nothing: the landing of tw, the clock behind a stall, the first rows and the last rows of a down stage, and the landing of rows in the first pair. All of them erred the same way, and the clock alone is 9.7 us in gate and up.

- **Matmuls removed, -59.9, and waits of 9.9:** right to within 7.5 us. With the ring and the queues out of the way (kernel 12) the two stages take 426.5, and 488.8 less 59.9 less 9.9 is 419.
- **Ring turn, 5.42 + L, L = 3.7:** right. The turn shown measures 9.16 with its L at 3.71, the mean in the second pair is 3.68. From row 6 to row 66 the second pair took 184.9 us; 60 rows at 3.04 and the 2.1 for pieces are 184.5.
- **Pieces, combines and splits in the first pair, 5.9 + 2.5:** nearly right in sum. Rows 6 to 66 took 193.9 for a forecast 190.8. By kernel 6 the 28 operand pieces are 2 of it (2.6 in these rows) and not the forecast 3.7, and the second pair's 184.9 has 2.5 for the 16 residual pieces. That leaves, as an estimate, 6 us for combinations, splits and a stretch of half clock (3.4 us long, at row 24), where the sum had 2.5; these were not taken apart.
- **First rows of a stage, missed.** Rows 0 to 6 were put at 18.8 us, plus 2 for t_scr's store; they took 25.5 and 22.0. The forecast saw one late split in row 1. It didn't count the five stores that stand between the loads of rows 2 and 3 in the changed queue. Terms: +4.7 and +3.2; kernel 8, which spreads these stores, brings the six rows to 17.2 and 17.1. Part of both terms is the clock behind the late row 3, which makes row 4 late: in the second pair the same program took 20.5 us for these rows in kernel 1, with no stretch of half clock, and 22.0 with one. The in-order wait of the first residual piece, not counted either, is worth at most 0.9 us by itself (kernel 7).
- **Last rows, missed.** "Residual sums (0.69) and squares fit into a row" looked at each engine's work, 1.23 + 0.68 us on VectorE and 1.04 + 0.63 + 0.19 on ScalarE in a row of 3.04. But they wait for each other in a circle of 3.57. Rows 66 to 76 took 37.0 and 33.0 for 30.4: +6.6 and +2.6. In the first pair an operand's split in the same programs and a half clock behind it are in the 6.6. Kernels 9 and 11, with four slots, removed all of it: rows 66 to 76 take 27.5 and 27.3 in 11. With these two points pair 0 is 244.8 + 4.7 + 3.1 + 6.6 = 259.2, and pair 1 is 236.5 + 3.2 + 0.4 + 2.6 = 242.7.
- **Sums in gate and up at nothing:** right, by kernel 1.
- **Late loads of tw, 5 x 2.2 = 11, at most 19:** the step that failed most, +16.2. Place, number and chain were as forecast, and with a landing of 5.65 (kernel 5) the idle time is 2.25 a block, the forecast's 2.2. But the text named "a 1 MB store behind" and still took 5.5 us; with it the load takes 6.8 to 7.8. That is the difference of 3.5 to 2.25 in idle time, 6.2 for five (0.3 more are 2.25 for 2.2). The other 9.7 are the granted clock, which no term of the sum knew. The upper end of 19 was too low for the same reason: it had the landing of 7.1, and no clock.
- **Tail, -0.6:** right; from the last matmul's start to the end of the span 11.3 us (2363.81 to 2375.1) for 11.9 (2321.58 to 2333.5).

The row gaps that were to tell short from long landing (3.0 and 3.2) came out at 3.1 and 3.3 from row 3 to row 76: the long landing's rival gave 2368 for a reason that holds in part, L at 4.0 in the first pair. None of the rivals had the clock or the ends of the stages in it.

## What to carry to other kernels

When a stage's steps are halved, look at its first and its last steps by themselves: whatever stands once in the queue there (stores, one wait in order, squares) had twice the time to hide before. Draw the waits between two engines as a circle and add up all of it; each engine's own load says nothing about it. And price a stall of TensorE with the clock that follows it: here five stalls of 3.5 us cost 5.4 each. Before a late row is put down to what its load waited for, see whether TensorE had a gap there at all (row 4). Where an edit moves work later, look at what else waits for that work on a queue (row 76).

## What the runs showed of the hardware

- At gaps of TensorE of 3.2 to 4.3 us in an otherwise busy stage the granted clock went down to half, for 3.4 or 6.8 us, with matmuls 0.427 us apart. It is not one to one: in the first pair's gate and up the changed kernel and kernel 3 each had five such gaps and four such stretches, and in both the shortest gap (3.20 and 3.18 us) had none; kernel 5, with gaps of 1.8 to 3.0 us, had one, at the gap of 3.0. In kernel 12 there was none between 989 us and the last matmul. Whether a stretch is 3.4 or 6.8 us long stays open: the same program had two of 6.8 in one run and one in the other.
- The down stages of the changed kernel had such stretches too, 13.7 us in the first pair (from 1454.2, 1525.9 and 1682.9 on) and 3.4 us in the second (from 2133.5 on), behind gaps of 3.8, 2.3, 2.4 and 2.2 us. These stages have more gaps than gate and up, and stretches came behind shorter ones. In kernel 1 the second pair's largest gap at its start is 1.8 us, and there is no stretch.
- The five late loads of 1 MB, with a store of 1 MB issued 0.5 us behind them (1.7 in one case), land in 7.1 us in the mean, and in 5.6 when the store is held back. So what is queued behind a transfer can lengthen it; by what means was not tried. The store is not all that counts: in kernel 1 the same loads stand behind a load of weights and ahead of stores of 256 KB, and land in 6.9 to 8.5 us. The Trainium skill (DMA: Bandwidth & Descriptors, section on queues, rings and completion order) says that each DMA engine takes up a ring's descriptors in order, and that a later one may finish its write before an earlier one. The trace agrees: of the transfers shown at the start of the first down stage the load issued at 1445.28 landed 5.9 us later, the 1 MB store issued ahead of it at 1444.75 took 6.8 and landed 0.4 us behind it.
- Two loads of 256 KB issued 0.38 us apart in the mean land 3.7 us after the first issue (second pair of the changed kernel), the same as one load of 512 KB in [rows 6, 7].
